# One block of keys at every second step: the weighing products of a stick-breaking attention

## The reference

```python
for blk in range(S // Q_BLOCK):                  # Q_BLOCK = 128
    t0 = blk * Q_BLOCK
    n_keys = t0 + Q_BLOCK
    z = jnp.einsum("bhtd,bhsd->bhts", qb, kb) * scale
    causal = s_pos < t_pos
    log_beta = jax.nn.log_sigmoid(z)
    log_keep = jnp.where(causal, jax.nn.log_sigmoid(-z), 0.0)
    between = lax.cumsum(log_keep, axis=3, reverse=True) - log_keep
    weights = jnp.where(causal, jnp.exp(log_beta + between), 0.0)
    outs.append(jnp.einsum("bhts,bhsd->bhtd", weights, vb))
```

## Time and profile before

| what | before |
|---|---|
| median of 3 runs | 2539.27 us (2537.24 to 2540.8) |
| the profiled execution | 2535.23 us |
| its span | 2533.5 us, mean granted clock of TensorE 0.999 |
| TensorE matmul busy | 2478.4 us (98%), 12076 instructions |
| TensorE weight load busy | 2024.0 us (80%) |
| VectorE busy | 1714.7 us (68%) |
| ScalarE busy | 1046.0 us (41%) |
| GpSimd busy | 149.4 us (6%) |
| the chain that ended last | TensorE 85%, VectorE 6%, DMA 4%, ScalarE 3% |

### The profile page before, as it was taken

The page is one execution under the profiler, slowest core; times in us unless marked ns, Lnnn a source line. Parts: engine busy times, 40 slices in busy tenths (PEclk is TensorE's granted clock), DMA queues, the critical chain, the costliest instruction groups (busy, mean ns, idle before and its releaser), DMA issues.

```text
span 2533.5 us, 33955 instructions
## 1 busy us (share of the span) xinstructions
PE 2478.4 (98%) x12076; PEld 2024.0 (80%) x12076; DVE 1714.7 (68%) x2150; ACT 1046.0 (41%) x1504; POOL 149.4 (6%) x155
## 2 busy tenths in 40 slices
PE   6999999999999999999999999999999999999999
PEld 4888888888888878888899888666688888888887
DVE  6978766658867656766642454777358787678884
ACT  5554342235554431111311235777435555533321
POOL 0000000000000000000000002566100000000000
PEclk9999999999999999999999999999999999999999
DMA  6334574213444475554143254665313555665333
GB/s 259 129 137 172 191 255 145 100 51 133 151 148 169 146 274 199 183 204 160 50 128 109 90 166 135 145 136 116 133 34 153 171 190 177 225 245 198 130 121 116
DMA packets 152747, 391.13 MB, mean 154 GB/s; under 512 B 13248, under 2 KB 41920, under 8 KB 148800
## 3 DMA queue, kind: packets, MB, share of 16 engines
q1 hardware_dynamic: 152640, 389.69, 45.6%
HBM read 285.83 MB, written 103.81 MB: 154 GB/s over the span
## 4 chain that ended last, share of the span: by engine, by line
PE 85%; DVE 6%; DMA 4%; ACT 3%; issue 1%; SPq 1%; DVEq 0%; ACTq 0%
PE PS L2463 24%; PE PS L2465 24%; PE PS L2464 24%; PE PS L3000 2%; PE PS L3015 2%; DVE KEEP L2384 2%; DMA MODRAW<-in_modw 2%; PE PS L2567 1%; PE PS L2569 1%; PE PS L2568 1%; PE PS L2980 1%; PE PS L2901 1%; PE PS L2981 1%; ACT PS L1541 1%; DMA MOD<-in_modw 1%
## 5 line engine op out<-in xcount | busy, mean ns | idle before, releaser
L2463 PE MATMUL PS<-H_HI,W_HI 128*128 128x512 f32 x700 | 277.0, 396 | 3.3 <-DVE H_LO L1664 2.2
L2465 PE MATMUL PS<-H_HI,W_LO 128*128 128x512 f32 x700 | 272.9, 390 | 0.0
L2464 PE MATMUL PS<-H_LO,W_HI 128*128 128x512 f32 x700 | 272.7, 390 | 0.0
L2463 PE MATMUL PS<-HID_HI,W_HI 128*128 128x512 f32 x640 | 250.9, 392 | 6.0 <-DVE HID_LO L1898 3.9
L414 ACT ACTIVATE W_HI<-RAW 128x1024 fp32r<-128x1024 f32 x90 | 93.9, 1057 | 381.2 <-PE PS L2465 291.1
L2465 PE MATMUL PS<-HID_HI,W_LO 128*128 128x512 f32 x640 | 249.1, 389 | 0.0
L2464 PE MATMUL PS<-HID_LO,W_HI 128*128 128x512 f32 x640 | 249.1, 389 | 0.0
L1720 DVE SCALAR_TENSOR_TENSOR X<-PS,MODV,X 128x1024 f32<-128x1024 f32 x76 | 97.4, 1282 | 126.2 <-PE PS L2465 122.7
L2384 DVE TENSOR_TENSOR_SCAN KEEP<-PS,MASK 128x1024 f32<-128x1024 f32 (+3 forms) x112 | 147.7, 1349 | 47.6 <-ACT PS L1541 38.5
L424 DVE SCALAR_TENSOR_TENSOR MODRAW<-MODRAW,PS 128x1024 f32<-128x1024 f32 x96 | 116.8, 1217 | 64.5 <-DMA MODRAW<-in_modw 64.1
L2463 PEld LDWEIGHTS PS<-H_HI,W_HI 128*128 128x128 f32 x700 | 131.5, 188 | 33.0 <-DVE H_LO L1664 4.3
(11 more groups left out here) (274 smaller groups left out, 5815.0 us busy)
## 6 DMA issues: line engine op xcount, KB each, us to landing
RAW<-in_wt SPq DMA_DIRECT2D x184, 512.0 KB, 4.2
MODRAW<-in_modw SPq DMA_DIRECT2D x96, 512.0 KB, 3.5
hid_scratch<-TN SPq DMA_DIRECT2D x66, 256.0 KB, 2.2
HRAW<-hid_scratch SPq DMA_DIRECT2D x8, 2048.0 KB, 9.3
hid_scratch<-SCR SPq DMA_DIRECT2D x60, 256.0 KB, 2.3
B_RAW<-block_scratch SPq DMA_DIRECT2D x15, 1024.0 KB, 7.8
X<-x_scratch SPq DMA_DIRECT2D x6, 2048.0 KB, 9.2
QK<-qk_scratch SPq DMA_DIRECT2D x16, 768.0 KB, 6.3
```

Source lines behind the costliest of these rows:

```text
L2463: pe.matmul(dst, w_hi, m_hi, start=first, stop=False)
L2464: pe.matmul(dst, w_hi, m_lo, start=False, stop=False)
L2465: return pe.matmul(dst, w_lo, m_hi, start=False, stop=last)
```

## The change

Before, two blocks are weighed at steps 1, 5, 9, 13, 17 and 21: at step 5 blocks 0 and 1, and so on to step 21 with 8 and 9. Blocks 10 and 11 are weighed at step 1 of the next pair. After, one block is weighed at every odd step: step 1 has block 11 of the pair before, step 3 block 0, step 5 block 1, and so on to step 23 with block 10. Behind the tail, one block is left to weigh where there were two.

```diff
-                    if n % 4 == 1 and back is not None:
-                        for q in (n // 2 - 2, n // 2 - 1):
-                            if q >= 0:
-                                weigh(back, q, b)
-                            elif before is not None:
-                                weigh(before, STEPS + q, 1 - b)
+                    if n % 2 and back is not None:
+                        q = n // 2 - 1
+                        if q >= 0:
+                            weigh(back, q, b)
+                        elif before is not None:
+                            weigh(before, STEPS + q, 1 - b)
...
             first_o(0)
-            weigh(Count(KT - 1), STEPS - 2, 1)
             weigh(Count(KT - 1), STEPS - 1, 1)
             first_o(1)
```

## The result

The changed kernel took 2577.09 us (median of 4 runs, 2573.4 to 2580.33) against 2538.91 us for the kernel before beside it. The ratio is 1.0152, 95% interval 1.0140 to 1.0164: slower by 38 us. The forecast was 2570, its range 2559 to 2583. The profiled execution took 2573.4 us, 38.2 us more than that of before.

The account below looks back on a forecast made before the run. TensorE was taken as nearly the bound of the attention loop, busy 28.32 of 30 us. Six pairs +26.3, first pair +2.3 and tail +2.4 made +31.0 us: 2570.3 from a median of 2539.27, range 2559 to 2583.

Parts of the forecast that it names:

- The waits: At steps 3 and 19, blocks 0 and 8 wait for OT_LO, 2.2 and 1.7 us; their stretches grow 2.0 and 1.8 us.
- The cost of a group: Weighing products on TensorE: each group costs 0.32 us, paid by the group, for 6 more groups a pair 1.9 us.
- Rival 1: Weighing groups: the waits hold but a group costs only 0.16 us more, about +22 us, 2561; chance 0.10.
- The anchors: Scores whose start a scan sets; step 13 to 16, held by the second head's scan 0, changes by 0.
- The clock: Attention loop on TensorE: the granted clock stays 1.00 from 1615 us on.
- rival 2: The new waits also lower the clock: +10 us if behind block 0's, 2580; behind block 8's too, 2590; chance 0.13.
- First pair and tail: Ends of the attention loop: first pair +2.3 us; tail +2.4 us, from five more groups 1.6 and block 8's wait 0.8.
- Rival 3: OT_LO ends before TensorE reaches blocks 0 and 8: 2531 to 2536, or 2544 with 0.32 us a group; chance 0.04.
- Rival 4: The waits at blocks 0 and 8 cost half through unseen slack behind them: about +15 us, 2554; chance 0.07.

Follow-up runs that it names:

- first experiment: The changed kernel with blocks 0 and 8 left where they were, at steps 5 and 21, ten groups a pair: 2549.64 us, ratio 1.0052.
- second experiment: The kernel before with only blocks 0 and 8 moved, to steps 3 and 19, eight groups a pair: 2555.36 us, ratio 1.0070.
- last experiment: The kernel before with its first two groups split, blocks 0 to 3 at steps 5, 6, 8 and 9: 2542.54 us, ratio 1.0017.
- tuned release: The changed kernel with ScalarE's raw copy freeing the PSUM bank, copies placed earlier and VectorE's OT_LO where it is idle: 2543.94 us, ratio 1.0023.
- third: The changed kernel with ScalarE copying the whole sum out to free the bank, OT_HI and OT_LO made from the copy: 2555.52 us, ratio 1.0071.

## Why the prediction was right, and where it was short

**The waits** were right in place, cause and size. They were forecast as 2.2 us at block 0 and 1.7 at block 8, and are 2.2 and 1.7. The stretches that hold them grew by 2.09 and by 1.87 to 1.95 us where 2.0 and 1.8 were forecast. The 0.1 us too little is in the restart: TensorE began 0.13 us behind OT_LO and not the 0.05 read from the earlier trace rows. The first experiment shows that these two blocks carry most of the loss: left where they were, they take 27 of the 38 us away. The second shows the part that they cost alone, 18 us, without a fall of the clock. The two halves, 11.9 and 17.6 us, and the 9.5 of the clock, which falls in neither, come to 39.0 us, about the whole of 38.

**The cost of a group** was right in kind and too high. It is paid by the group and not by the block: 0.23 us in the changed kernel (step 4 to 13, two groups, 0.46 us), 0.25 and 0.30 in the first and the last experiment, 0.32 in the prediction. The Trainium skill (TensorEngine Tiling, Key Properties) says that a change of the tiling mode drains TensorE; a price for entering and leaving the products of 64 columns agrees with it, but no run here takes a drain apart from another cause. Without the waits, the twelve groups cost 0.5 us a pair net of the idle time that they fill. Rival 1 is excluded, as its 0.16 us lies below all three. Its sum was also wrong: with half of the 0.32 going with the block, each of the eight groups of one block costs 0.08 us less and not 0.16, 0.64 us a pair and not 1.28, so that it stood near 2565 (an estimate) and not at 2561.

**The anchors** held: step 13 to 16 stayed at 4.32 us to the hundredth, because the scan sets it.

**The clock** is the step of the forecast that failed. "The granted clock stay 1.00 from 1615 on" was wrong, and rival 2, at a chance of 0.13, was what happened, on top of the forecast's mechanism. It was put at +10 us for one fall a pair. It measures 1.58 us a fall and 9.5 us for six falls; its 2580 is nearer to the 2577 than the forecast's 2570. The argument against it was that TensorE works without a pause before and behind the wait, unlike in the first pair. The changed kernel shows that this doesn't protect it: the clock fell behind four of six waits of 2.2 us and two of six of 1.7, while behind 1.7 and 1.2 us, in the second experiment, it never did. Filling the same waits removed the falls and the time. So the waits bring the falls, but what decides behind which of them the clock falls stays open; that the falls of this trace come to one a pair, as rival 2 had it, is an average over six pairs. The Trainium skill (TensorE: Matmul & The Clock Gate, Why this matters for your kernels) names idle gaps between bursts of matmuls as what brings the half rate. The trace agrees for six of these gaps, and for six others of the same lengths it shows the full rate. The total came within 7 us of the forecast because the waits and groups, 4.23 us a pair where 4.4 stood, were right; the range held the result because its upper end was set for this rival.

**First pair and tail.** At the end of the first pair the changed kernel is 2.3 us later, as forecast, but by luck. In this execution its first score starts 2.2 us earlier than in that of before (1576.34 against 1578.58), and the pair itself takes 4.5 us more. 1.2 of these lie ahead of every weighing, in the products of L2901 (2.9 us in place of 1.7, at a mean clock of 0.57 in place of 1.00). The tail came to +1.1 us and not +2.4. Its wait at block 8 is 0.78 us (0.8 forecast), and its five groups come to 1.25 at 0.25 each, an estimate, and not to 1.6. By that, what lies before block 8 is 0.9 us shorter than forecast. Step 1 weighs one block less there (0.4 us), which I had left out; the rest I didn't follow up.

**Rival 3** (OT_LO ahead of TensorE) did not occur by itself. The tuned release makes it happen, and gives +6 us: 2543.94, near that rival's 2544 for the full group cost, though the group costs less than it had.

**Rival 4** (half-cost waits) is excluded by the table.

## What to carry to other kernels

A piece of work that is moved earlier takes its waits with it: list what it waits for, and find the time at which each is released in the present trace. If that time is later than the new place, the move stalls the engine, whatever idle time it was meant to fill. Free the resource first (here a PSUM bank, by the copy that comes soonest), and then move. A stretch without a wait may owe that to the work in it, so before you take work out, ask what the next instruction would then meet.

## What the runs showed of the hardware that was not expected

- TensorE's granted clock fell to half behind six of twelve waits of 2.2 and 1.7 us in an otherwise busy stream, and took 1.58 us from the pair each time. Six matmuls of discarded work (1.4 us) inside each wait kept it at 1.00. A pair then took 1.72 us less, 10.3 us over six.
- A VectorE subtraction of 128x512 with both inputs in SBUF took 1.82 us (from 1705.04) when GpSimd had begun its own at 1704.85, which ran to 1706.32. It took 0.67 us (from 1715.49) when it was ahead of GpSimd's by 0.24 us, and then that one, of 128x1024, took 2.17 us and not the 1.90 of the kernel before. With one input in PSUM it took 0.66 or 0.67 us in the loop of every kernel here that does it so, also beside GpSimd (1675.25 before, where GpSimd's from 1675.50 took 1.90). The Trainium skill (GPSIMD Engine Reference, Specifications) says that GpSimd shares its SBUF interfaces with VectorE and contends with instructions of two SBUF inputs; the trace agrees.
- A weighing product started 0.12 to 0.13 us behind its releaser after waits of 2.16 us (1691.56), 1.22 us (second experiment) and 0.33 us (third), and 0.05 us behind it when discarded work stood right ahead, with 0.68 us still to wait. So it isn't the length of the wait; what it is isn't shown.
